# One core, six layers: another order for ScalarE's copies in two delta-rule recurrences, and for the key rotations of a sparse attention

## The reference, cut to what matters

```python
# rwkv7_time_mix, shifted = tokens moved by one
xm = h[:, :, None, :] + (shifted - h)[:, :, None, :] * mix          # six mixes
decay = exp(-exp(-softplus(-(w0 + tanh(xw @ w1) @ w2)) - 0.5))
a = sigmoid(a0 + (xa @ a1) @ a2)
g = sigmoid(xg @ g1) @ g2                                           # g1: 1024 x 160
v = v + (v_first - v) * sigmoid(v0 + (xv @ v1) @ v2)                # second RWKV layer alone
state = state * w_t - sa * (kk_t * a_t) + v_t * k_t                 # per token, 16 heads of 64x64
y_t = state @ r_t
```

```python
# dsa_attention
q = rope(rms_norm(q, q_norm), pos); k = rope(rms_norm(k, k_norm), pos)
# scores of an index head choose 64 keys per query; softmax over them; @ v
```

## Time and profile before

| | us |
|---|---|
| median of 3 runs (1948.94 to 1954.17) | 1950.82 |
| the profiled execution | 1942.91 |
| its span on the core | 1940.8 |
| its mean granted TensorE clock | 0.97 |

### The profile page before, as it was taken

The page is one execution under the profiler, slowest core; times in us unless marked ns, Lnnn a source line. Parts: engine busy times, 40 slices in busy tenths (PEclk is TensorE's granted clock), DMA queues, the critical chain, the costliest instruction groups (busy, mean ns, idle before and its releaser), DMA issues.

```text
span 1940.8 us, 41718 instructions
## 1 busy us (share of the span) xinstructions
PE 1823.6 (94%) x17879; PEld 1633.6 (84%) x17879; DVE 1220.0 (63%) x1783; ACT 1045.7 (54%) x1623; POOL 68.2 (4%) x58
## 2 busy tenths in 40 slices
PE   6987999999989999898999999988999999998998
PEld 5887888889979888797698898777798888887887
DVE  7834367864436775485778856745367755775764
ACT  5844465555535554354655546744555544565455
POOL 0000100000000000113000000000100000000000
PEclk8988999999989999899999999999999999999998
DMA  6420065557567555355475562410065555443541
GB/s 193 131 78 6 3 198 186 186 185 248 175 219 228 195 188 188 116 163 182 131 202 195 189 195 83 131 59 3 4 196 194 190 179 164 149 133 105 163 131 66
DMA packets 288526, 287.75 MB, mean 148 GB/s; under 512 B 15240, under 2 KB 286456, under 8 KB 288344
## 3 DMA queue, kind: packets, MB, share of 16 engines
q1 hardware_dynamic: 285048, 283.98, 45.7%
q10 hardware_dynamic: 3296, 1.11, 0.3%
HBM read 284.03 MB, written 1.05 MB: 147 GB/s over the span
## 4 chain that ended last, share of the span: by engine, by line
PE 88%; DVE 4%; ACT 4%; issue 2%; DMA 1%; POOL 0%; SPq 0%; DVEq 0%; ACTq 0%; POOLq 0%
PE ps L412 23%; PE ps L413 12%; PE ps L389 10%; PE ps L390 9%; PE ps L391 9%; PE ps L812 2%; PE ps L429 2%; PE ps L430 2%; PE ps L431 2%; PE ps L708 1%; PE ps L788 1%; PE ps L670 1%; PE ps L797 1%; PE ps L636 1%; ACT wh L446 1%
## 5 line engine op out<-in xcount | busy, mean ns | idle before, releaser
L456 DVE TENSOR_TENSOR wl<-raw,wh 128x1024 fp32r<-128x1024 f32 x484 | 586.2, 1229 | 421.1 <-ACT wh L446 416.3
L446 ACT ACTIVATE wh<-raw 128x1024 fp32r<-128x1024 f32 x484 | 499.5, 1041 | 491.7 <-PE ps L391 221.2
L412 PE MATMUL ps<-HH,wh 128*128 128x512 f32 x1408 | 489.7, 391 | 0.0
L413 PE MATMUL ps<-HH,wl 128*128 128x256 f32 x1408 | 397.0, 282 | 0.0
L412 PEld LDWEIGHTS ps<-HH,wh 128*128 128x128 f32 x1408 | 264.3, 188 | 55.6 <-issue 0.4
L389 PE MATMUL ps<-HH,wh 128*128 128x256 f32 x928 | 271.8, 293 | 12.5 <-DVE HH L2545 6.2
L413 PEld LDWEIGHTS ps<-HH,wl 128*128 128x128 f32 x1408 | 266.1, 189 | 0.1
L390 PE MATMUL ps<-HH,wh 128*128 128x256 f32 x928 | 263.1, 284 | 0.0
L391 PE MATMUL ps<-HH,wl 128*128 128x256 f32 x928 | 262.5, 283 | 0.0
L389 PEld LDWEIGHTS ps<-HH,wh 128*128 128x128 f32 x928 | 179.0, 193 | 22.8 <-issue 4.6
L390 PEld LDWEIGHTS ps<-HH,wh 128*128 128x128 f32 x928 | 178.9, 193 | 1.3 <-issue 1.2
(11 more groups left out here) (323 smaller groups left out, 2990.3 us busy)
## 6 DMA issues: line engine op xcount, KB each, us to landing
raw<-in_ffn_w_gu_dram SPq DMA_DIRECT2D x88, 1024.0 KB, 5.1
raw<-in_ffn_w_down_dram SPq DMA_DIRECT2D x32, 1024.0 KB, 5.1
raw<-in_w_in_dram SPq DMA_DIRECT2D x32, 1024.0 KB, 5.7
raw<-in_rw_w_rkv_dram SPq DMA_DIRECT2D x24, 1024.0 KB, 5.3
B<-in_w_ada_dram SPq DMA_DIRECT2D x24, 1024.0 KB, 7.8
raw<-in_ds_w_in_dram SPq DMA_DIRECT2D x14, 1024.0 KB, 5.0
raw<-in_ffn_w_down_dram SPq DMA_DIRECT2D x16, 768.0 KB, 4.4
raw<-in_sb_w_qkv_dram SPq DMA_DIRECT2D x12, 1024.0 KB, 5.3
```

The costliest lines, as they stand in the source:

```text
L412: e.matmul(o[:, m, :], h_[:, k, c], x_, start=k0 + k == 0, stop=False, skip_group_check=True)
L413: i = e.matmul(o[:, m, 0:S], l_[:, k, c], x_[:, 0, :], start=False, stop=k0 + k == kt - 1, skip_group_check=True)
L446: e.activation(wh[:, u % UNITS, 0:kn * 256], raw[:, j % RAW, k0 * 256:(k0 + kn) * 256], ACT.Copy).then_inc(*up("hi"))
L456: e.tensor_tensor(wl[:, u % UNITS, 0:kn * 256], raw[:, j % RAW, k0 * 256:(k0 + kn) * 256], wh[:, u % UNITS, 0:kn * 256].bitcast(F32), ALU. ...
```

## The change

1. RWKV, copies: in each level ACT copies `turned` right after `xs`, and makes its two units behind them (one of them ahead of the next level's copies); one unit fewer is made ahead of the levels and one more behind. DVE's `level("low")` comes ahead of the decays, `own_term` and `value_mix`. `value_rates` (the 16 products of `v2`, n=1) move from between the halves of the last read block into the first level, and its sigmoids behind that level's copies. `bp` moves between the halves. Bank counting goes on from `full(0,1,2)`. In m = 32 `pTM` comes ahead of the second products, on PE and ACT. The grams `br`, `kr` and the `term` products change places with transposes.
2. Early factors (n=0): `w1` and `a1` have a semaphore apart from `g1`, and their mixes stand ahead of `h` on DVE. ACT does `wa` first, then `prepare(1)`, and `prepare(0)` comes behind the first key block, on DVE behind the running sums.
3. One-pass columns: `gv` becomes one product of `h` with both column groups side by side (`gt`), an ACT copy to `lor`, and two products with the identity, the second a token later.
4. Sparse attention: rope q3 before the key norm, k0 and k1 behind v1, k2 and k3 behind v2, nothing behind v3. Modulation block 11 moves from between the heads to behind the last value product, its turn behind the output projection. SP's loads for blocks 8 and 9 wait for less.

```diff
 def load_down(e, n):
+    for name, a, z, landed_ in (("rw_w1", 0, 64, s_down), ("rw_a1", 64, 128, s_down), ("rw_g1", 128, 256, s_down_g)):
...
 # pe_rwkv
-            pe_lora(e, ("gv", n), tail, tail_mixed, 0, 64 if n else 32, h, ("dve", ("lora tail", n)))
+            tw = 32 + 32 * n
+            o = bank(e, ("gt", n), ("act", ("gt", n)))
+            for k in range(KD):
+                i = e.matmul(o[0:2 * tw, 0:S], tail[:, k, 0:2 * tw], h[:, k, :], start=k == 0, stop=k == KD - 1, ...)
             full(0, 1, 2)
+            o = bank(e, ("gv", n), ("act", ("gv", n)))
+            e.wait_ge(*at("act", ("gt", n)))
+            e.matmul(o[0:tw, 0:S], ident[0:2 * tw, 0:tw], lor[0:2 * tw, :], start=True, stop=False, ...)
+            e.matmul(o[0:tw, 1:S], ident[0:2 * tw, tw:2 * tw], lor[0:2 * tw, 0:S - 1], start=False, stop=True, ...)
...
+            last_read = block_halves(0, 1, 3)
+            cur["first"], cur["bank"] = 1, bank_of["full", n, 0, 2]
             for j in range(2):
                 gram("pb", j, Pm, Bt_)
+            next(last_read)
+            for j in range(2):
+                gram("bp", j, Bt_, Pm)
...
                 second_products(LEVELS[g])
+                if n and g == 0:
+                    value_rates()
                 next(values)
             first_products(32)
             for j in range(2):
                 gram("kp", j, Kp, Pm)
-            second_products(32)
-            cur["first"] = 0
             for j in range(2):
                 pe_to_tm(e, ("pTM", n, j), Pm, j)
+            second_products(32)
...
 # act_rwkv
-            prepare(0, XH)
+            if n:
+                prepare(0, XH)
+            else:
+                prepare(1, HH)
+                hi(e)
...
+            e.wait_ge(*at("mm", ("gt", n)))
+            e.activation(lor[0:2 * tw, :], PS("gt", n)[0:2 * tw, 0:S], ACT.Copy).then_inc(...)
+            hi(e)
+            evac(0, 2, R_)
             e.wait_ge(*at("mm", ("gv", n)))
             e.activation(sg[0:32, 1, :], PS("gv", n)[0:32, 0:S], ACT.Sigmoid).then_inc(...)
...
+            hi(e, 1)
             for g in range(4):
+                hi(e, 1)
+                if g == 0:
+                    evac(0, 3, R_)
+                elif n == 0:
+                    evac(2, g - 1, v_)
                 for j in range(2):
                     quarters_out("xs", LEVELS[g], j, X1)
+                turned(LEVELS[g] // 2)
+                if g == 2:
+                    ... # the eye copy, ahead of the levels before
                 hi(e, 1)
-                turned(LEVELS[g] // 2)
-                hi(e, 1)
+                if n and g == 0:
+                    ... # sigmoids of v2
...
 # dve_rwkv
             for g in range(4):
-                if n and g:
-                    value_mix(g - 1)
+                lo(e, 1)
+                level("low", LEVELS[g], T)
                 lo(e, 1)
                 ... # decays, own_term
-                level("low", LEVELS[g], T)
-                lo(e, 1)
+                if n:
+                    value_mix(g)
...
 # pe_dsa, at its end
+            rope("q", q_, 3)
             norm("k", FM(7))
+            for i in range(1, 4):
                 tm_block(e, ("ds", "v", i), h, None, ("act", ("ds", "v", i)))
-                rope("k", k_, i - 2)
-            rope("k", k_, 2)
-            rope("k", k_, 3)
+                if i < 3:
+                    rope("k", k_, 2 * i - 2)
+                    rope("k", k_, 2 * i - 1)
```

More of the change, by code:

```diff
@@ L171, in build @@
         s_rows = [sem(f"s_rows{i}") for i in range(3)]
-        s_down, s_tail, s_lora_up, s_v2 = (sem(f"s_{n}") for n in ("down", "tail", "lora_up", "v2"))
+        s_down, s_down_g, s_tail, s_lora_up, s_v2 = (sem(f"s_{n}") for n in ("down", "down_g", "tail", "lora_up", "v2"))
         def C(name, a=0, b=None):
@@ L521, in build @@
         down, down_mixed = (BUF[i][:, :].rearrange("p (k n) -> p k n", k=KD) for i in (9, 10))
[L522 removed]
+        tail = BUF[12][:, 1024:2048].rearrange("p (k n) -> p k n", k=KD)
         lora_up, v2_up = BUF[6][:, 1024:2048], v2_rows[32:64, :]
         def load_down(e, n):
[L526 to L527 removed]
+            for name, a, z, landed_ in (("rw_w1", 0, 64, s_down), ("rw_a1", 64, 128, s_down), ("rw_g1", 128, 256, s_down_g)):
+                e.dma_start(down[:, :, a:z], wview(A[name][n])[:, :, 0:z - a]).then_inc(landed_, 16)
         def load_tail(e, n):
@@ L841, in second_products, with value_rates @@
                         quarters("low", m, j, Tw, X1, "dve")
[L843 to L850, removed]
+            def value_rates():
                 e.wait_ge(*at("act", ("gv", n)))
@@ L858, in pe_rwkv @@
                     i.then_inc(*up("mm", ("v2", n, g)))
+            last_read = block_halves(0, 1, 3)
+            cur["first"], cur["bank"] = 1, bank_of["full", n, 0, 2]
+            for j in range(2):
+                gram("pb", j, Pm, Bt_)
             next(last_read)
+            for j in range(2):
+                gram("bp", j, Bt_, Pm)
+            for _ in last_read:
+                pass
             for g in range(4):
@@ L868, in pe_rwkv @@
                 gram("kp", j, Kp, Pm)
-            second_products(32)
-            cur["first"] = 0
             for j in range(2):
                 pe_to_tm(e, ("pTM", n, j), Pm, j)
-            for j in range(2):
-                gram("br", j, Bt_, R_)
+            second_products(32)
+            cur["first"], cur["bank"] = 0, bank_of["tt", n, 32, 1, 1] + 1
             e.wait_ge(*at("dve" if n else "act", ("vmix", n, 3) if n else ("full", n, 2, 3)))
@@ L878, in pe_rwkv @@
             for j in range(2):
-                gram("kr", j, Kp, R_)
+                gram("br", j, Bt_, R_)
             for j in range(2):
@@ L889, in pe_rwkv @@
                 pe_to_tm(e, ("kTM", n, j), Kp, j)
+            for j in range(2):
+                gram("kr", j, Kp, R_)
+            for g in range(4):
+                o = bank(e, ("term", n, g), ("act", ("term", n, g)))
+                e.wait_ge(*at("dve", ("term", n, g // 2)))
+                e.matmul(o[:, :], C("bones"), term[:, 2 * g:2 * g + 2, :], start=True, stop=True, skip_group_check=True).then_inc(*up("mm", ("term", n, g)))
             for j in range(2):
@@ L902, in pe_rwkv @@
                                 i.then_inc(*up("mm", ("tp", n, j, a)))
[L904 to L907, removed]
             jg, g2 = raw_piece(e)
@@ L1568, in act_rwkv @@
             evac(1, 0, k_)
+            if n == 0:
+                prepare(0, XH)
+                hi(e)
             log_and_exp(e)
@@ L1576, in act_rwkv @@
             for g in range(1, 4):
-                hi(e)
+                if n or g < 3:
+                    hi(e)
                 evac(1, g, k_)
@@ L1662, in act_rwkv @@
                 to_tm(("kTM", n, j), kTM[:, j, :])
+            for g in range(4):
+                e.wait_ge(*at("mm", ("term", n, g)))
+                e.activation(term[:, 2 * g:2 * g + 2, :], two(PS("term", n, g)[:, :]), ACT.Copy).then_inc(*up("act", ("term", n, g)))
             for j in range(2):
@@ L1666, in act_rwkv @@
                     copy_out(("tp", n, j, a), TP[:, 2 * j + a, :])
-            for g in range(4):
-                e.wait_ge(*at("mm", ("term", n, g)))
-                e.activation(term[:, 2 * g:2 * g + 2, :], two(PS("term", n, g)[:, :]), ACT.Copy).then_inc(*up("act", ("term", n, g)))
             def negate_u(c):
```

128 lines of the change are left out of this document (76 added, 52 removed).

## The result

The changed kernel takes 1902.19 us, median of 4 runs (1894.99 to 1904.63), against 1950.23 of the kernel before: ratio 0.9744, 95% interval 0.9712 to 0.9776, or 48 us. 1896 was forecast. The profiled execution took 1904.63, its span is 1902.6, 38.2 less than that of before.

The account below looks back on a forecast made before the run. PE was taken as the bound (88% of the chain), losing time to waits and low clock. Terms of -60.1, +3 for the clock at `gv` and +2 for small waits gave -55: 1888 profiled, 1896 median, range 1880 to 1922.

Parts of the forecast that it names:

- the main case: Whole run: waits for turned copies go, a level takes 12.06 us, median 1896 (1882 to 1908), chance 0.69.
- the displaced DVE work fills its idle time: Levels: `level("low")` ahead of decays and `value_mix` only makes DVE's release earlier; no gain counted for it.
- the early factors: Front of n=0: `wa` starts 5.5 us earlier, but ACT paces the key blocks; no separate gain, bounds 0 and -8.
- the one-pass columns: `gv` by `gt` ahead of `pb`: gain nothing, as DVE paces the block behind and `pb` waits for the sigmoid.
- the wait at the start: PE's 7.0 us wait for the mixed factors in n=0 shrinks to about 2.
- the wait for the sigmoid in n=0: At `pb`, sharing `gv`'s bank: it starts 3.4 us after the block's end; new wait of 2.5 to 3.8 us.
- the sparse attention: Start of the attention: PE's 8.2 us wait for POOL becomes 1.9 for ACT, 6.3 less; bounds 8.2 and 3.
- +0.7: n=1, stretch up to `pb`: 0.7 us slower, as `pb` takes `gv`'s own bank and waits for its sigmoid.
- the front of n=0: Up to `pb`: read block 2 starts at 83.1, ends at 88.9, `pb` at 92.3 against 91.34, so +0.9 us.
- m = 32: Stage after the levels: `pTM` ahead gives ACT time for copies; 10.8 and 11.6 us, so -3.5 (n=0) and -2.8 (n=1).
- +3 for the clock at `gv`: Both layers: gaps of about 3 us at `gv` where the clock can fall, +3 us together, bounds 0 and 6.
- The rule on the shared port: Sparse attention: DVE and POOL operations exclude each other, giving 8.9 us per block, 1.4 above PE's; +3 for two, not summed.

Follow-up runs that it names:

- The filled waits: The kernel before, with eleven identity products on PE in place of each of the eight waits, copies as late as before: 1933.43 us, ratio 0.9927.
- its reordering: Kernel after with pb's bank moved on in n=0 and, on DVE, m = 32 copies ahead of last value mix, own term and rest: 1890.5 us, 0.9726.
- the bank free: Kernel after with n=0's banks counted one further from `pb` on, so its first is not `gv`'s: 1892.03 us (0.9724), again 1898.62 us (0.976).
- the repeat: The changed kernel itself, unchanged, run once more on the chip of other follow-up kernels: 1895.68 us, ratio 0.9768 to the kernel before.
- run 13: Not a run's number but part of "made the run 13 us faster": kernel before with identity products in place of the eight waits, 1933.43 us, 0.9927.

## Why the prediction was right, and where a step failed

**Right:** the main case. The turned copies end before the half block, PE is the only limit, and a level is 12.02 us (forecast 12.06). The filled waits show both halves of the price: 20 us of waiting and 11.3 of low clock, of which 5.4 in n=0, where I had put the whole rest of 6.9 down to the clock. What I had wrong is by which edit: the order on ACT alone gives 22 us in the two windows, out of 29 to 32, and the rest, for which I counted nothing ("the displaced DVE work fills its idle time"), goes with DVE's order and the move of `v2`. Its rows were the 7.59 us of DVE in a level: a load under the limit says nothing on whether its one awaited piece comes first. (Two slips of no effect: 131.66 - 124.72 is 6.94 and not 6.75, and 128.3 + 2.04 lies 5.6 and not 5.8 us into the level.)

**Right:** no gain to speak of from the early factors and the one-pass columns; the wait at the start (1.7 left for about 2), that of PE at the key norms (4.3 for about 5), the wait for the sigmoid in n=0 (2.4; 3.4 from the block's end to `pb`, as forecast), and the sparse attention (-6.5 for -6.3, 1.7 of wait left for 1.9).

**Failed:** "+0.7" in n=1 with "1 + 3 % 7 = 4, `gv`'s own bank". I took n=1's banks from the kernel before. The new resets of the counter shift them: counted through the code it is 7 for `full(0,1,2)`, 0 for `gv`, 1 for `pb`, and no wait stands there. In n=1 the stretch from the key blocks to `pb` got 1.3 us shorter.

**Mis-sized:** the front of n=0, +3.0 for +0.9. I put read block 2 at 83.1; it starts at 85.15, 1.4 us after PE is free, for DVE's `lo` behind four parts of `erase_and_write`: DVE is busy 5.00 of 5.07 us there (the row 80.08 above). The term was named but its time taken too early: these parts start only at 79.00, when ACT's L1589 has released them. That DVE sets this start, and not PE, the run with the early factors undone shows, where `gt` begins 1.15 us sooner (78.93 for 80.08) and the block only 0.4.

**Mis-sized:** m = 32, +1.4 and -1.5 for -2.8 and -3.5. The step that failed is that "`pTM` ahead of the second products gives ACT time for the copies". I took PE's idle time in the stage, 14.25 - 10.78, for waits for ACT's copies. In n=0 the waits view of before names none there:

```profile
PE ps L812 <- issue: 1.8, 1, 1.8
PE ps L722 <- issue: 1.4, 1, 1.4
PE ps L788 <- DVE B L2305: 0.3, 1, 0.3
```

In n=0 after, a gap at "issue" of 1.6 us and 0.4 of waiting for DVE stay, with the 10.7 of PE nearly the whole 12.71. In the eight other traces with this order of PE and `gt` the gap stands ahead of the same product, the fourth from the end of `second_products`, with 1.0 to 1.6 us; in the two without `gt` it stands 11 products earlier, with 0.7. So it goes with a place in PE's program and not with DVE's order; its cause is open. In n=1 DVE's own term, value mix and rest ahead of the copies cost 2.2 us, as its reordering shows; the clock fell there in the profiled execution, which is another 2, and 1.3 us are gaps at "issue".

**Mis-sized:** +3 for the clock at `gv`. Behind `gv` it fell for 3.4 us in n=0 only, and the row 94.36 has 11.47 for the 10.05 that the same work takes with the bank free: 1.4. It fell for longer where I had no term, behind the key norms (6.8 us, n=0).

**The reference.** The sum stood against an execution 8 us quicker than its median. On the spans I forecast 55 less and 38 came, or 47 with the repeat's span of 1894.2; on the medians 48. Of the 17 that are missing 8.3 lie in stretches for which I had forecast nothing, 5.6 of them in the last line of the table. The levels and m = 32 of n=1 were 5.4 longer than in the repeat of after. So the stages gave less than I added up, and a part of the hit is luck: where the clock falls differs between executions of one kernel by as much as the terms that I got wrong.

**The rule on the shared port.** POOL's rotation after, two per value block (timeline, POOL):

```profile
887.00 1.28 POOL L2881 TENSOR_TENSOR B<-B 128x512 f32<-128x512 f32 x1
888.36 2.14 POOL L2884 TENSOR_TENSOR B<-B 128x512 f32<-128x512 f32 x1
890.46 2.27 POOL L2881 TENSOR_TENSOR B<-B 128x512 f32<-128x512 f32 x1
...
895.43 2.13 POOL L2884 TENSOR_TENSOR B<-B 128x512 f32<-128x512 f32 x1
```

and DVE's `lo` between 887 and 896 us:

```profile
887.38 1.98 DVE L456 TENSOR_TENSOR wl<-raw,wh 128x1024 fp32r<-128x1024 f32 x1 [1.18 <-ACT wh L446]
...
894.78 1.66 DVE L456 TENSOR_TENSOR wl<-raw,wh 128x1024 fp32r<-128x1024 f32 x1 [1.99 <-ACT wh L446]
```

POOL's operations take 1.28 us alone and up to 2.27 beside DVE's `lo`, and the `lo` take 1.76 on the mean there, 1.23 alone. So POOL's last add ends at 897.56, just 0.5 us ahead of ACT's copy, which ends at 898.06: the order has hardly any slack left. The Trainium skill, page "SBUF — State Buffer", section "SBUF: two separate sides", says that such a pair of operations exclude each other, the loser waiting for the whole instruction. The trace agrees: the add that starts at 895.43 meets a `lo` that ends at 896.44, and 896.44 + 1.28 is 897.72, where it ended at 897.56; the `lo` of 887.38 meets a multiply that ends at 888.28, and 888.28 + 1.23 is 889.51, where it ended at 889.36. The prediction read 2.17 against "2.5" as agreeing in part, but a duration holds only the rest of the other's instruction, not a full turn. The +3 us did not come. I had put DVE's sine parts, which read PSUM and one buffer, into the same queue; two of them take 1.28 us beside POOL's multiply at 891.51, as they do at 884.92, mostly alone. Without them the queue is 5.0 and 2.5, no longer than PE's 7.5 for a block, and PE waited for neither.

## What to carry to other kernels

Put an engine's copies that another engine waits for directly behind their source, on every engine of the ring: ACT's order alone gave 22 of the 29 to 32 us of the levels, as DVE's copies were the next to be waited for. A wait of 2.5 us in PE's work cost another 1.4 us of low clock on average, so that eight of them cost 31 us where the waits view shows 20. Before idle time is put down to a wait, read in the waits view what ended it: at m = 32 of n=0 it was no copy of ACT's. Before a bank is named in an argument, count the banks of the new kernel, for each layer, and before an early start is costed, look for the engine that is full between it and the end.

## What was not expected of the hardware

Useless products in the place of a wait made the run 13 us faster (0.9927, 0.9903 to 0.9951). And the same gap does not always lower the clock: between two executions of one kernel, a stretch of 53 us differed by 2 us, most of it in this way (PE busy 53.97 and 52.27 us), and where the clock rises at the start moved the key blocks of n=0 by up to 3.9 us (32.98 and 36.87) between executions with the same code up to there. Gaps of 1.0 to 1.6 us that wait for nothing shown stood ahead of the same product in nine traces.
